# Expert gate and up products with the weights as stationary operand, 80 tokens moving

## The reference, cut to what matters

```python
def expert_choice_ffn(h, w_router, w_gate, w_up, w_down):
    aff = jax.nn.softmax(jnp.dot(xs, w_router).astype(jnp.float32), axis=-1)
    cap = EC_FACTOR * n // N_EXPERTS
    gates, idx = lax.top_k(aff.T, cap)
    xe = xs[idx]
    hid = jax.nn.silu(jnp.einsum('ecd,edf->ecf', xe, w_gate)) * jnp.einsum('ecd,edf->ecf', xe, w_up)
    ye = jnp.einsum('ecf,efd->ecd', hid, w_down) * gates[..., None].astype(h.dtype)
    out = jnp.zeros_like(xs).at[idx.reshape(-1)].add(ye.reshape(-1, D))
```

## Time and profile before

| | us |
|---|---|
| median of 3 runs | 1894.52 |
| lowest and highest | 1892.17, 1896.10 |
| the profiled execution, its own time | 1889.44 |
| its span, first to last instruction | 1887.7 |
| TensorE matmul busy | 1794.9 (95%) |
| TensorE weight load busy | 973.2 (52%) |
| VectorE / ScalarE / GpSimd busy | 815.6 / 316.3 / 200.5 |

### The profile page before, as it was taken

One profiled execution on the slowest core, in us unless ns is written; L12 is line 12 of the kernel. 1 busy time (PEld: TensorE's weight loads), 2 busy tenths in 40 slices (PEclk: granted clock), 3 DMA queues, 4 the chain that ended last, 5 costly groups with the idle time before them and its releaser, 6 DMA issues. The chain is left out here.

```text
span 1887.7 us, 33944 instructions
## 1 busy us (share of the span) xinstructions
PE 1794.9 (95%) x14602; PEld 973.2 (52%) x14602; DVE 815.6 (43%) x1746; ACT 316.3 (17%) x680; POOL 200.5 (11%) x275
## 2 busy tenths in 40 slices
PE   5999989988999999999889999899799999999996
PEld 2455655443466565445345666554435655653553
DVE  2335876254242424343343458843534342424241
ACT  2223643120000000000032245521200000000000
POOL 1004200000000000000010142000000000000000
PEclk9999999999999999999999999999999999999998
DMA  9860020358999999999985300331699999999993
GB/s 385 311 234 1 1 109 32 163 208 346 395 410 398 408 401 409 404 405 401 392 316 218 134 0 1 109 133 69 250 390 408 401 398 398 401 396 406 399 404 116
DMA packets 56213, 526.70 MB, mean 279 GB/s; under 512 B 12046, under 2 KB 13694, under 8 KB 26142
## 3 DMA queue, kind: packets, MB, share of 16 engines
q1 hardware_dynamic: 40494, 375.60, 49.8%
q10 hardware_dynamic: 9312, 128.45, 16.1%
q0 software_dynamic: 6336, 21.63, 4.6%
HBM read 503.91 MB, written 24.38 MB: 280 GB/s over the span
## 5 line engine op out<-in xcount | busy, mean ns | idle before, releaser
L643 PE MATMUL PS<-arena,xe 128*32 128x512 f32 x3456 | 384.9, 600 | 11.4 <-DMA arena<-w_exp 7.6
L643 PE MATMUL PS<-ada,xe 128*32 128x512 f32 x2688 | 294.4, 592 | 4.2 <-DVE RA L1491 4.2
L643 PEld LDWEIGHTS PS<-arena,xe 128*32 128x32 f32 x3456 | 168.0, 111 | 214.2 <-issue 175.2
L659 PE MATMUL PS<-arena,hdT 128*32 128x512 f32 x1536 | 268.0, 596 | 5.6 <-DVE RA L1511 3.9
L661 PE MATMUL PS<-arena,hdT 128*32 128x256 f32 x1024 | 264.7, 381 | 0.0
L643 PEld LDWEIGHTS PS<-ada,xe 128*32 128x32 f32 x2688 | 130.5, 110 | 158.7 <-issue 121.9
L1168 ACT ACTIVATE RA<-PS 128x768 f32<-128x768 f32 x32 | 25.9, 810 | 975.5 <-PE PS L643 975.5
L1478 DVE STREAM_TRANSPOSE RA<-RA 32x256 f32<-32x256 f32 x384 | 167.1, 435 | 40.5 <-DMA RA<-normed_rows,idx_g 34.8
L703 PE MATMUL PS<-arena,RB 128*128 128x512 f32 (+1 forms) x480 | 183.4, 530 | 0.0
L1491 DVE TENSOR_TENSOR RA<-RA,PS 128x768 f32<-128x768 f32 x32 | 30.5, 954 | 339.4 <-ACT RA L1168 339.4
L664 PE MATMUL PS<-arena,hdT 128*32 128x256 f32 x1536 | 157.8, 381 | 0.0
(11 more groups left out here) (293 smaller groups left out, 1846.1 us busy)
## 6 DMA issues: line engine op xcount, KB each, us to landing
arena<-w_exp SPq DMA_DIRECT2D x76, 2048.0 KB, 20.9
arena<-w_exp ACTq DMA_DIRECT2D x60, 2048.0 KB, 14.2
ada<-w_exp SPq DMA_DIRECT2D x56, 2048.0 KB, 21.4
arena<-ada_rest SPq DMA_DIRECT2D x16, 2048.0 KB, 9.2
ada<-ada_first SPq DMA_DIRECT2D x8, 2048.0 KB, 33.8
arena<-w_in SPq DMA_DIRECT2D x4, 2048.0 KB, 10.1
arena<-w_out SPq DMA_DIRECT2D x2, 4096.0 KB, 12.7
arena<-w_in SPq DMA_DIRECT2D x4, 1536.0 KB, 18.8
```

Source lines behind the costliest of these rows:

```text
L643: last = mm(PS[GRP * q:GRP * (q + 1), g * 512:(g + 1) * 512], xe[:, k, GRP * g:GRP * (g + 1)], w[:, q, :], start=(k == 0), stop=(k == KD - ...
L659: mm(PS[GRP * q:GRP * (q + 1), 1536:2048], tok(q), w[:, 0:512], start=first, **flags)
```

## The change

The gate and up products take the weights as the stationary operand: a 128x128 block of weights is loaded, and the 80 tokens of the expert move past it, for 8 blocks `f` of gate and 8 of up columns, and 8 blocks `k` of inputs. The result lies in PSUM as the turned hidden tile, FF on the partitions and the tokens on the columns, 80 to a block, so nothing is turned afterwards: `hidden_turned` and its semaphore `hd_rdy` go, and `down` waits for `hm_rdy`. The hidden tile has two buffers (`hdT`, and a piece of `RA`), used in turn, so the loops on ScalarE and VectorE go over pairs of experts. `down` keeps its form and moves to banks 4 and 5. The 16 unused columns of both hidden buffers are cleared once a layer, in place of those of `xe`, and behind a wait for the stores of the normalised rows (`stored`). The weights are laid out otherwise in HBM, with the same sizes of transfers.

```diff
-        hid = RA[:, 2 * D:2 * D + MAIN].rearrange("p (g c) -> p g c", g=3)
+        hidden = [hdT[:, :, :], RA[:, 2 * D:2 * D + KD * PAD].rearrange("p (j s) -> p j s", j=KD)]
+        hid = [h[:, :, 0:SLOT].rearrange("p (b j) s -> p b j s", b=2) for h in hidden]
...
-            return w.rearrange("p (c n) -> p c n", c=4)
+            return w.rearrange("p (f n) -> p f n", f=16)
...
+        def gu_view(up):
+
+            return PS[:, 1024 * up:1024 * (up + 1)].rearrange("p (b c) -> p b c", b=2)[:, :, 0:4 * SLOT].rearrange("p b (j s) -> p b j s", s=SLOT)
...
                     w = gate_up_weights(k, other)
-                    for g in range(3):
-                        for q in range(4):
-                            last = mm(PS[GRP * q:GRP * (q + 1), g * 512:(g + 1) * 512], xe[:, k, GRP * g:GRP * (g + 1)],
-                                      w[:, q, :], start=(k == 0), stop=(k == KD - 1), skip_group_check=True)
+                    for f in range(16):
+                        o = (f // 4) * 512 + (f % 4) * SLOT
+                        last = mm(PS[:, o:o + SLOT], w[:, f, :], xe[:, k, 0:SLOT],
+                                  start=(k == 0 and f % 4 == 0), stop=(k == KD - 1), skip_group_check=True)
...
-            def down(E):
+            def down(E, odd):
+
                 pe.wait_ge(ys_rdy.sem, E + 1)
-                pe.wait_ge(hd_rdy.sem, E + 1)
+                pe.wait_ge(hm_rdy.sem, E + 1)
...
-                    tok = lambda grp: hdT[:, k, GRP * grp:GRP * (grp + 1)]
+                    tok = lambda grp: hidden[odd][:, k, GRP * grp:GRP * (grp + 1)]
...
-            def silu_gate(E):
+            def silu_gate(E, odd):
                 act.wait_ge(gu_used.sem, 4 * E + 4)
-                if not isinstance(E, int) or E:
-                    act.wait_ge(hd_rdy.sem, E)
-                A(hid, PS[:, 0:1536].rearrange("p (g c) -> p g c", g=3)[:, :, 0:REST], ACT.Silu).then_inc(sg_rdy.sem, 1)
+                A(hid[odd], gu_view(0), ACT.Silu).then_inc(sg_rdy.sem, 1)
...
-                V.tensor_tensor(hid, hid, PS[:, 0:1536].rearrange("p (g c) -> p g c", g=3)[:, :, REST:512], ALU.mult).then_inc(hm_rdy.sem, 1)
-
-            def hidden_turned(E):
-
-                dve.wait_ge(hm_rdy.sem, E + 1)
-                dve.wait_ge(dn_used.sem, 2 * E + 1)
-                V.transpose(hdT[:, :, :].rearrange("p b (g s) -> p g b s", g=3),
-                            hid.rearrange("p g (b r) -> p g b r", r=GRP)).then_inc(hd_rdy.sem, 1)
+                V.tensor_tensor(hid[odd], hid[odd], gu_view(1), ALU.mult).then_inc(hm_rdy.sem, 1)
...
-                V.memset(xe[:, :, SLOT:PAD], 0.0)
+                dve.wait_ge(stored.sem, stored.at(l, 2 * NT))
+                for h in hidden:
+                    V.memset(h[:, :, SLOT:PAD], 0.0)
...
                     tokens_turned(loop, l, e + 1)
                     column(loop, l, e + 2, 1, idx_g[:, :], idx_rdy)
-                    times_up(E)
+                    times_up(E, odd)
                     tokens_in(E)
-                    hidden_turned(E)
                     rows_out(l, e - 1, E - 1)
                     loop.end()
```

More of the change, by code:

```diff
@@ L366, in build @@
         hm_rdy = Signal("hm_rdy", EXP)
-        hd_rdy = Signal("hd_rdy", EXP)
         ys_rdy = Signal("ys_rdy", EXP, primed=True)
@@ L656, in down @@
                     first = k == 0
-                    tok = lambda grp: hdT[:, k, GRP * grp:GRP * (grp + 1)]
+                    tok = lambda grp: hidden[odd][:, k, GRP * grp:GRP * (grp + 1)]
                     for q in range(3):
-                        mm(PS[GRP * q:GRP * (q + 1), 1536:2048], tok(q), w[:, 0:512], start=first, **flags)
+                        mm(PS[GRP * q:GRP * (q + 1), 2048:2560], tok(q), w[:, 0:512], start=first, **flags)
                     for grp in range(2):
-                        mm(PS[96:P, 1536 + grp * REST:1536 + (grp + 1) * REST], tok(grp), w[:, MAIN:D],
+                        mm(PS[96:P, 2048 + grp * REST:2048 + (grp + 1) * REST], tok(grp), w[:, MAIN:D],
                            start=first and grp == 0, **flags)
                     for q in range(3):
-                        mm(PS[GRP * q:GRP * (q + 1), 2048:2304], tok(q), w[:, 512:MAIN], start=first, **flags)
-                    last = mm(PS[96:P, 2048:2304], tok(2), w[:, MAIN:D], start=first, **flags)
+                        mm(PS[GRP * q:GRP * (q + 1), 2560:2816], tok(q), w[:, 512:MAIN], start=first, **flags)
+                    last = mm(PS[96:P, 2560:2816], tok(2), w[:, MAIN:D], start=first, **flags)
                     if k % 4 == 3:
@@ L1107, in _ @@
                     gate_up(l, 2 * i + 1, True, i)
-                    down(E - 1)
+                    down(E - 1, 0)
                     pe.wait_ge(hm_rdy.sem, E + 1)
                     gate_up(l, 2 * i + 2, False, i + 1)
-                    down(E)
+                    down(E, 1)
                 pe.wait_ge(hm_rdy.sem, hm_rdy.at(l, EXP - 1))
                 gate_up(l, EXP - 1, False, N_A - 1)
-                down(l * EXP + EXP - 2)
+                down(l * EXP + EXP - 2, 0)
                 pe.wait_ge(hm_rdy.sem, hm_rdy.at(l, EXP))
@@ L1119, in _ @@
                     first_modulation(l + 1, range(4))
-                down(l * EXP + EXP - 1)
+                down(l * EXP + EXP - 1, 1)
                 if l + 1 < LAYERS:
@@ L1390, in down_parts @@
                                       ).then_inc(ewd_in[j].sem, 16)
[L1392 to L1396, removed]
+                silu_gate(l * EXP, 0)
+                with act.Fori(0, N_B) as i:
+                    E = l * EXP + 2 * i
+                    silu_gate(E + 1, 1)
+                    down_parts(E + 1)
+                    silu_gate(E + 2, 0)
+                    down_parts(E + 2)
+                silu_gate(l * EXP + EXP - 1, 1)
+                down_parts(l * EXP + EXP - 1)
         @block.vector
@@ L1487, in tokens_in, with times_up @@
                 shifted_in(xq_view)
-            def times_up(E):
+            def times_up(E, odd):
                 dve.wait_ge(sg_rdy.sem, E + 1)
-                V.tensor_tensor(hid, hid, PS[:, 0:1536].rearrange("p (g c) -> p g c", g=3)[:, :, REST:512], ALU.mult).then_inc(hm_rdy.sem, 1)
-            def hidden_turned(E):
-                dve.wait_ge(hm_rdy.sem, E + 1)
-                dve.wait_ge(dn_used.sem, 2 * E + 1)
-                V.transpose(hdT[:, :, :].rearrange("p b (g s) -> p g b s", g=3),
-                            hid.rearrange("p g (b r) -> p g b r", r=GRP)).then_inc(hd_rdy.sem, 1)
+                V.tensor_tensor(hid[odd], hid[odd], gu_view(1), ALU.mult).then_inc(hm_rdy.sem, 1)
             def rows_out(l, e, E):
@@ L1506, in rows_out @@
                 dve.wait_ge(dn_used.sem, 2 * E + 3)
-                V.scalar_tensor_tensor(ys[:, 0:MAIN], PS[0:SLOT, 1536:1536 + MAIN], gcur[0:SLOT, 0:1], g2r[:, 0:MAIN],
+                V.scalar_tensor_tensor(ys[:, 0:MAIN], PS[0:SLOT, 2048:2048 + MAIN], gcur[0:SLOT, 0:1], g2r[:, 0:MAIN],
                                        ALU.mult, ALU.mult)
                 for g, n in enumerate((GRP, GRP, CAP_C)):
-                    o = 1536 + g * REST
+                    o = 2048 + g * REST
                     ins = V.scalar_tensor_tensor(ys[GRP * g:GRP * g + n, MAIN:D], PS[PAD:PAD + n, o:o + REST], gcur[PAD:PAD + n, g:g + 1],
@@ L1937, in _, with one_expert @@
                 tokens_in(l * EXP)
-                times_up(l * EXP)
-                hidden_turned(l * EXP)
+                times_up(l * EXP, 0)
                 first.end()
-                with dve.Fori(1, EXP) as e:
+                def one_expert(e, odd):
                     E = l * EXP + e
@@ L1945, in _ @@
                     column(loop, l, e + 2, 1, idx_g[:, :], idx_rdy)
-                    times_up(E)
+                    times_up(E, odd)
                     tokens_in(E)
-                    hidden_turned(E)
                     rows_out(l, e - 1, E - 1)
                     loop.end()
+                with dve.Fori(0, N_B) as i:
+                    one_expert(2 * i + 1, 1)
+                    one_expert(2 * i + 2, 0)
+                one_expert(EXP - 1, 1)
                 if l + 1 < LAYERS:
@@ L2134, in expert_slabs @@
     u = w_up.reshape(n, 4, 2, P, FF).transpose(0, 1, 3, 2, 4)
-    d = w_down.reshape(n, 4, KD, GRP, D).transpose(0, 2, 1, 3, 4).reshape(n, 2, 4, P, D).transpose(0, 1, 3, 2, 4).reshape(n, 2, P, 4096)
-    gu = np.concatenate([w[..., q * REST:(q + 1) * REST] for q in range(4) for w in (g, u)], axis=-1)
+    d = w_down.reshape(n, 2, 4, P, D).transpose(0, 1, 3, 2, 4).reshape(n, 2, P, 4096)
+    gu = np.concatenate([g, u], axis=-1)
     return np.concatenate([gu.reshape(n, 4, P, 4096), d], axis=1).reshape(n, 6 * P, 4096)
```

## The result

The changed kernel takes 2222.28 us (median of 4 runs, 2218.92 to 2226.39) against 1895.31 before: ratio 1.1729, 95% interval 1.1704 to 1.1755. Forecast were 2135 and 2113 to 2153. The direction was right, the size was not: 87 us are missing.

What follows compares the result with a forecast made beforehand. TensorE sets the pace, with DMA near its limit. Load-bound gate_up adds 255.0 us; less 10.8, 0.6, 1.2 and 1.7, plus 0.3, gives +241.0: span 2128.7, time 2135 us, range 2113 to 2153.

Steps and rivals of the forecast that it cites:

- The clock: Rival: thinly streaming gate_up passes lose the 2.4 GHz clock; some 3050 us at 1.2 GHz throughout, 2590 half the time; chance 0.04.
- The pass: In gate_up, each of 256 passes is set by its weight load, 111.6 ns; +255.0 us over 32 experts.
- Stream-bound: Rival: in gate_up the load hides under the previous stream, 74 ns a pass; about 1892 us; chance 0.05.
- in-series: Rival: in gate_up load and stream follow one another, 179 ns a pass; about 2690 us; chance 0.02.
- The borders: Between gate_up and down: only a few ns more per expert, allowed for in the upper bound; period 38.9 us.
- (a): Last expert of layer 0: its late weights and slow clock no longer lengthen its period, -10.8 us.
- (b): Second gate_up of each layer: shorter wait for silu and product, -0.3 us each, -0.6 in all.
- (c): Last down of layer 1: VectorE's turning of the hidden tile, 1.22 us, goes; -1.2 us, bounds 0 and -3.9.
- (d): Last down of layer 0: its wait for weights behind a DMA backlog goes, -1.7 us, bounds 0 and -1.7.
- What costs nothing: Other transposes, second hidden buffer, bank change, pair loops and stores wait: no time; two memsets replacing one, +0.3 us in all.
- the first case: The forecast itself, gate_up passes bound by their loads at full clock: 2135 us, range 2113 to 2153, chance 0.89.

Runs made afterwards that it cites:

- Experiments 2 and 3: Changed kernel with 128 (2) or 96 (3) columns instead of 80 moving past each load, the added results unread: 2149.90 and 2147.23 us.
- kernel 6: Changed kernel with four unread matmuls in each idle stretch before each layer's first and second gate_up, eight fewer in an earlier filler: 2143.83 us.
- experiment 1: Changed kernel with four unread 320-column matmuls in each idle stretch before the first and second gate_up of each layer: 2344.24 us.

## Why the prediction was wrong

The step that failed is the rival called "The clock", in two ways. Its price was for the low clock throughout (3050) or half the time (2590), and I gave it 0.04, so that the sum had the clock's loss at nothing; what happened is a third case that I hadn't laid out, three streams of 32, 80 us. And its "Against it" carried, transposes with 128 columns, back to back, over to passes with 80 columns in 112 ns. Experiments 2 and 3 show that this can't be carried over: with 128 and with 96 columns the clock comes back inside gate_up, with 80 it did not in 54 us. The trigger stood in the trace of before: TensorE is idle 2.12 us after the first gate_up of each layer, and 1.9 us before it, in this row of its waits (both layers together). The clock fell at the latter and was at 0.50 for about the first 3.4 us of the first gate_up of both layers, which costs half of that, 1.7 us; the window is layer 1's, and I did not read it for what comes after it:

```profile
PE PS L643 <- DVE xe L1467: 3.8, 2, 1.9
```

```profile
1367.40:1370.80 3.40, 3.40 (x20) 0.81 (x24) 0.00 (x0) 0.00 (x0) 1.11 (x2) 0.50 0.99 424
```

The change takes away the dense stream that ended such a fall. The Trainium skill, "TensorE: Matmul & The Clock Gate", section "HAM oscillation — how this bites in real kernels", tells of a kernel that waits some 3 to 5 us for a DMA between bursts of matmuls and starts each burst at the low clock, and it reckons half of the time at the low clock as lost. The trace agrees on the price (54.48 us for a stream of 28.54) and that idle time comes first, but here that was 1.90 us, shorter than the section's, and the loss went on for 54.6 us of gapless passes, which the section doesn't have.

The sum, term by term:

- The pass: right. 111.6 ns forecast, 111.7 measured; both neighbours in the earlier trace rows gave it, and the transposes of the earlier trace rows did not mislead. The Trainium skill's columns / 1.2, 107 ns for 128 columns (same page, section "LDWEIGHTS (loading the stationary operand)"), is 5 ns short of it. Stream-bound and in-series are out, the latter against the Trainium skill's section "The mechanism" on that page: loads and streams overlap here though they use the same rows, 112 ns a pass where one after the other would be 179.
- The borders: mis-sized. gate_up and down were summed to 38.9; the period is 39.24, gate_up reaching 28.75 to the start of down and down 10.49 instead of 10.32. The difference is 0.35 us an expert, about 10.5 in 30 periods, and the starts in the trace place it where one form of load gives way to the other: 174 ns from the first pass to the second, 205 from the last one to `down`, 309 from the last matmul of `down` to the next gate_up, where it is 112 inside gate_up and 193 to 240 between groups inside `down`. It accounts for most of why kernel 6, with no clock lost, has a span of 2139.7 and not 2128.7. Why a change of form costs this was not tried.
- (a) right: the last expert of layer 0 takes a normal period, 10.8 us back.
- (b) right within 0.1: 1.90 instead of 2.12 us of wait.
- (c) right as a number, by luck. The turned tile's 1.22 us went, and the rows were out at 2187.97 + 1.50 = 2189.47, which would have made the forecast wait of 2.7 us; but the last down of layer 1 then waited 1.1 us more for its own weights, so 3.72 against 3.88 in the earlier trace rows. What did come back is clock, which I had put at nothing: the last down ran at 0.50 for 3.4 us instead of 5.3, worth 0.9. Both rows are of the kernel after:

```profile
2187.97 1.50 DVE L1512 SCALAR_TENSOR_TENSOR RA<-PS,gcur,RA 32x256 f32<-32x256 f32 x3
...
2190.55 0.77 PE L664 MATMUL PS<-arena,RA 128*32 128x512 f32 x3 [3.72 <-DMA arena<-w_exp]
```

- (d) nearly right: all waits on `w_exp` together are 4.1 us, 3.72 of them the row above, so 0.4 remain of 1.69.
- What costs nothing: right, nothing of it shows. The DMA share fell less than forecast: 338 GB/s at a share of 0.94, where 404 had 1.01.

Together 2128.7 + 10.5 + 80.2 (the three long periods over their normal length) + 1.3 for (d) = 2220.7, against 2217.0 measured; the 3.7 between them are not accounted for. The range failed for one reason: it was the first case's own range, on the strength of the 0.04. With the clock kept, kernel 6, the time is 2143.83 and lies in it.

## What to carry to other kernels

A float32 matmul with a full load and few moving columns (here up to 128) costs its weight load; read the distance of starts in two neighbouring shapes, and if it doesn't change with the columns, it is the load. When a change thins TensorE's stream, look for every idle stretch behind which the dense stream used to get the clock back, and price each as a whole stream at half clock; fill the stretch, or widen the moving operand where the load leaves room. Filler and finer pieces add instructions: watch the instruction queue's packets when a loop grows, or when code ahead of it does.

## What the runs showed that was not expected

- Eight matmuls a layer outside the loop (experiment 1) cost 122 us against the changed kernel instead of saving some 78, since the loop's instructions were loaded again in layer 1: 110 packets against 56.
- Two loads of 64 columns into two column groups take under 70 ns together, one of 128 columns 112 ns.
- The two layers run identical code, yet the fall comes before the second gate_up in layer 0 and before the first in layer 1; in the kernel before it comes before the first in both, and the 2.12 us stretches pass without one. What decides whether a given idle stretch of 1.9 us lowers the clock stays open.
